# Queries and keys of the second mixer projected with seven products for eight, in a two-layer diffusion backbone

## What is computed

```python
mod = silu(c) @ w_mod + b_mod                 # 1024 x 6144, for c and for c_ctx
h = x * (1 + sc1) + sh1
qa, ka, va, qb, kb, vb, qc, kc, vc = split(h @ w_in)   # nine parts, one matrix
oa, ob, oc = diff_attend(qa, ka, va), neighbourhood_attend(qb, kb, vb), gqa_attend(qc, kc, vc)
ga, gb, gc = split(sigmoid(h @ w_gate + b_gate))
y = (ga * (oa @ w_br[0]) + gb * (ob @ w_br[1]) + gc * (oc @ w_br[2])) @ w_o
x = layernorm(alpha * x + g1 * y); then a mixture of experts, and layernorm again
```

## Time and profile before

| | us |
|---|---|
| median of 3 runs | 2131.27 (2130.95 to 2136.01) |
| profiled execution | 2136.38 |
| its span | 2134.3 |
| PE busy | 2007.2 (94%) |
| DVE busy | 1292.1 (61%) |
| granted clock of TensorE, mean | 0.984 |

### The profile page before, as it was taken

The page is one execution under the profiler, slowest core; times in us unless marked ns, Lnnn a source line. Parts: engine busy times, 40 slices in busy tenths (PEclk is TensorE's granted clock), DMA queues, the critical chain, the costliest instruction groups (busy, mean ns, idle before and its releaser), DMA issues. The chain is left out here.

```text
span 2134.3 us, 25339 instructions
## 1 busy us (share of the span) xinstructions
PE 2007.2 (94%) x9546; PEld 1173.9 (55%) x9546; DVE 1292.1 (61%) x2031; ACT 513.9 (24%) x1007; POOL 238.2 (11%) x250
## 2 busy tenths in 40 slices
PE   7999999999999999699899999999999999979995
PEld 3457766566467754344244676656755676434432
DVE  2747747675456665756444574776744665866664
ACT  2114401143124400122130342003402342002221
POOL 1000020421110000100120002031101000010003
PEclk9999999999999999899999999999999999989998
DMA  7631046411120061689781111552111105238996
GB/s 284 243 118 40 21 143 222 138 55 44 40 82 21 33 279 79 247 341 362 257 278 48 64 41 64 195 185 87 48 57 46 43 21 221 105 133 322 385 350 199
DMA packets 62682, 317.00 MB, mean 149 GB/s; under 512 B 14824, under 2 KB 15280, under 8 KB 34272
## 3 DMA queue, kind: packets, MB, share of 16 engines
q1 hardware_dynamic: 32688, 232.41, 28.9%
q0 software_dynamic: 13136, 53.64, 7.7%
q10 hardware_dynamic: 16736, 29.32, 3.8%
HBM read 286.70 MB, written 27.07 MB: 147 GB/s over the span
## 5 line engine op out<-in xcount | busy, mean ns | idle before, releaser
L1217 PE MATMUL ps<-ring,hT 128*128 128x512 f32 (+1 forms) x960 | 388.4, 560 | 4.0 <-DVE hT L2190 2.0
L1217 PE MATMUL ps<-ring,zT 128*128 128x512 f32 (+2 forms) x992 | 317.5, 600 | 2.0 <-ACT zT L2093 2.0
L1217 PE MATMUL ps<-R,ring 128*128 128x512 f32 (+2 forms) x1024 | 292.3, 437 | 6.3 <-DVE zT L2522 3.5
L1217 PEld LDWEIGHTS ps<-ring,hT 128*128 128x128 f32 x960 | 179.4, 191 | 187.4 <-issue 176.7
L1217 PE MATMUL ps<-hT,ring 128*128 128x320 f32 x896 | 260.5, 436 | 0.0
L1217 PEld LDWEIGHTS ps<-R,ring 128*128 128x128 f32 x1024 | 161.9, 191 | 118.0 <-issue 92.8
L1217 PEld LDWEIGHTS ps<-ring,zT 128*128 128x128 f32 (+2 forms) x992 | 121.5, 156 | 149.0 <-issue 146.4
L1217 PEld LDWEIGHTS ps<-hT,ring 128*128 128x128 f32 x896 | 164.8, 190 | 65.2 <-issue 2.6
L2370 DVE SCALAR_TENSOR_TENSOR R<-ring,cs,R 128x2048 f32<-128x2048 f32 x70 | 173.3, 2476 | 8.3 <-DMA ring<-in_wall 5.5
L2025 ACT COPY R<-ps 128x512 f32<-128x512 f32 (+2 forms) x170 | 96.1, 565 | 271.3 <-PE ps L1506 253.8
L1445 PE MATMUL ps<-R 64*128 64x128 f32 (+2 forms) x992 | 123.2, 374 | 5.7 <-ACT R L1896 2.5
(11 more groups left out here) (335 smaller groups left out, 2460.8 us busy)
## 6 DMA issues: line engine op xcount, KB each, us to landing
ring<-in_wall SPq DMA_DIRECT2D x188, 1024.0 KB, 6.0
hT<-in_wall SPq DMA_DIRECT2D x20, 1024.0 KB, 8.9
y_all<-R ACTq DMA_DIRECT2D x27, 512.0 KB, 6.9
R<-in_wall SPq DMA_DIRECT2D x10, 1024.0 KB, 9.0
R<-in_rows POOLq DMA_DIRECT2D x2, 4096.0 KB, 17.9
R<-mrows POOLq DMA_DIRECT2D x16, 512.0 KB, 21.5
R<-in_x ACTq DMA_DIRECT2D x10, 512.0 KB, 8.9
h_rows<-R ACTq DMA_DIRECT2D x10, 512.0 KB, 2.6
```

The lines of the kernel that those rows point to most:

```text
L1217: ins = nc.tensor.matmul(out, w, m, start=start, stop=stop, **kw)
```

## The change

Chunks 3 and 4 are now computed by the same scheme of seven products: four pairs of output tiles (`TURNED_PAIRS`), each with seven products of four steps in seven separate uses of six PSUM banks (`TURNED_BANKS`). GpSimd makes the four weight sums of a pair (`sum_turned`), in place or in free state, alternating between two sets. ScalarE copies the first product and the sum with the third, VectorE adds the others (`add_turned`, six additions). The token differences are those of the first mixer in `SG`.

The second mixer's gates need them afterwards in the kept slots: six transfers from GpSimd's queue now copy them there, where `token_sum` computed them. ScalarE waits for the transfers before it writes to `SG`.

Group 1 of the modulation gets an accumulator of its own (`first_acc`). Its first seven half passes are made in the merge of the first mixer, 20 more between the additions of the turned products, and the remaining five of group 2 behind them. The pieces' order is 4 behind chunk 3 and 4 behind chunk 4. Its sum is taken after the last turned pair.

The gates' weight sums are now taken one at a time (`one_sum`), at most two per slot of the attention, after an earlier product than before; the fourth is written into the weights themselves.

```diff
@@ -54,6 +54,8 @@
 ADDS = 6
 SUMS = 4
 SIGMOIDS = 3
+DIFFERENCES = 6
+MOST_SUMS = 2
 PIECE = 2048
 FAR = -1e30
 TIE = 1e-30
@@ -62,11 +64,12 @@
 MOD_GROUPS = D * 6 // 2048
 CHUNKS = {0: (2, 0, 1), 1: (3, 4, 5), 2: (6, 7)}
 CHUNK_TYPE = ("q", "k", "v", "q", "k", "v", "q", "kv")
-MOD_ORDER = ((2, 6, 0), (0, 0, 8))
-MOD_SUMS = ((4, 1), (5, 3))
+MOD_ORDER = ((4, 4, 0), (0, 0, 8))
+MOD_SUMS = ((4, 3), (5, 3))
+FIRST_SUMMED = 3
 NEXT_PASSES = {(2, 0): (0, 1, 2), (0, 0): (3,), (0, 1): (4,), (0, 2): (5,), (0, 3): (6,), (1, 0): (7,)}
 NEXT_SUM, NEXT_TURN, NEXT_COPY = (1, 1), (1, 2), (1, 3)
-PROJECT_SLOTS = (0, 1, 2, 3, 4, 5) + 3 * (2, 3) + (0, 1) + 4 * (2, 3)
+PROJECT_SLOTS = (0, 1, 2, 3, 2, 3, 4, 5, 2, 3, 2, 3, 0, 1) + 4 * (2, 3)
 def wall_order():
...
+TURNED_PAIRS = 4
+TURNED_BANKS = (2, 3, 2, 4, 5, 0, 1)
 def units(c):
...
     cross_sum = sb("cross_sum", [128, 4, 128])
+    turned_sums = [[a.rearrange("p (k n) -> p k n", k=4) for a in (area(13824, 512), area(14336, 512), area(17664, 512))],
+           [cross_sum[:], *(a.rearrange("p (k n) -> p k n", k=4) for a in (area(12800, 512), area(13312, 512)))]]
     cexp = area(18176, KB * 32).rearrange("p (k n) -> p k n", k=KB)
     lnst = area(26112, 16 * NT).rearrange("p (t a) -> p t a", t=NT)
...
@@ -626,23 +631,48 @@
     class SumsDone:
-      def __init__(self, first, last):
-        self.first, self.last, self.done = first, last, [[0, 0] for _ in range(3)]
-      def upto(self, br, n):
-        done = self.done[br]
-        while True:
-          a, b = done
-          if a > b:
-            if SEVEN * b + CROSS + 1 > n:
-              return
-            self.last(br, b)
-            done[1] += 1
-          else:
-            if a == PAIRS or (a and SEVEN * (a - 1) + LATE + 1 > n):
...
+        while most and self.done[br] < SUMS * PAIRS:
+          p, j = divmod(self.done[br], SUMS)
+          if n < (SEVEN * p + LOW_LOW + 1 if j == SUMS - 1 else SEVEN * (p - 1) + ACROSS + 1 if p else 0):
+            return
+          self.one(br, p, j)
+          self.done[br] += 1
+          most -= 1
+    def turned_pieces(layer, q):
...
             for dst, a, b in token_halves(layer, br, j):
               ch.step(nc.gpsimd.tensor_tensor(dst, a, b, ALU.subtract), g_tok)
+          def sum_turned(q):
+            for i in turned_pieces(layer, q):
+              pool.wait_ge(full[slot_of(layer, i)], 16 * loads_by(layer, i))
+            if q >= 2:
+              pool.wait_ge(pe_acc, turned_no(q - 2, HIGH_HIGH))
+            (a11, a12), (a21, a22) = turned_weights(layer, q)
+            both, cross, far = turned_sums[q % 2]
+            ch.step(nc.gpsimd.tensor_tensor(both, a21, a22, ALU.add), g_turn)
+            ch.step(nc.gpsimd.tensor_tensor(cross, both, a11, ALU.subtract), g_turn)
...
@@ -1082,9 +1125,15 @@
               if layer == 0:
                 zero_row = y_all[0:1, :].rearrange("r (p n) -> (r p) n", p=8)
                 pool.dma_start(zero_row, MB[0:8, 0, MB_ZERO[0]:MB_ZERO[0] + 128]).then_inc(zero_out, 16)
+              sum_turned(0)
+              pool.wait_ge(pe_gate, gate_no(0, PAIRS - 1, LATE))
               for g in range(LAT):
                 masked_bias(0, g)
+              pool.wait_ge(v_z, KB)
+              sum_turned(1)
               load_bias(1)
...
@@ -1098,12 +1147,13 @@
                 n = pieces.index((layer, ("in", 4, 1)))
                 pool.wait_ge(freed, taken_by(layer, n)[1])
                 for j in range(4):
-                  token_sum(1, j)
-              i = PU.index((br, c, CTX))
+                  for k0, k1, dst in token_rows(layer, 1, j):
+                    pool.dma_start(dst, token_rows(layer, 0, j)[0][2][:, 320 * k0:320 * k1]).then_inc(t_moved, 16)
+              i = PU.index((br, c, 0 if turned(c) else CTX))
               typ = CHUNK_TYPE[c]
               if typ == "k" and turned(c):
-                pool.wait_ge(a_copy, AU.index(PU.index((br, c, units(c) - 1))) + 1)
+                pool.wait_ge(v_turn, turned_adds(TURNED_PAIRS - 1, HIGH_HIGH))
                 pool.dma_start(OUT["bk"][layer].rearrange("p (b t) -> p b t", b=4), KT[:, :, LTOK:TOK]).then_inc(new_k_out, 16)
                 pool.wait_ge(new_k_out, 16 * (br + 1))
...
+          def turned_pair(q):
+            for h in range(2):
+              take("in", h)
+            (a11, a12), (a21, a22) = turned_weights(layer, q)
+            both, cross, far = turned_sums[q % 2]
+            copied = AU.index(PU.index((1, 3, 0))) + 2 * q
+            for o in range(SEVEN):
+              if o == LOW_LOW:
+                if q:
+                  pe.wait_ge(a_copy, copied)
+                weights, tokens = a11, lambda k: hT[:, k, early]
+              elif o == CROSS:
+                if q:
+                  pe.wait_ge(v_turn, turned_adds(q - 1, CROSS))
+                pe.wait_ge(g_turn, SUMS * q + 2)
+                weights, tokens = cross, lambda k: token_row(layer, 0, 1, k)
+              elif o == HIGH_LOW:
+                pe.wait_ge(a_copy, copied + 1)
+                weights, tokens = a12, lambda k: hT[:, 4 + k, early]
+              elif o == DOWN:
+                if q:
+                  pe.wait_ge(v_turn, turned_adds(q - 1, DOWN))
+                pe.wait_ge(g_turn, SUMS * q + 3)
+                weights, tokens = a21, lambda k: token_row(layer, 0, 2, k)
+              elif o == ACROSS:
+                if q:
+                  pe.wait_ge(v_turn, turned_adds(q - 1, ACROSS))
+                weights, tokens = both, lambda k: token_row(layer, 0, 0, k)
+              elif o == LATE:
+                if q:
+                  pe.wait_ge(v_turn, turned_adds(q - 1, LATE))
+                else:
+                  pe.wait_ge(v_z, KB)
+                pe.wait_ge(g_turn, SUMS * q + 4)
+                weights, tokens = far, lambda k: hT[:, 4 + k, late]
+              else:
+                if q:
+                  pe.wait_ge(v_turn, turned_adds(q - 1, HIGH_HIGH))
+                weights, tokens = a22, lambda k: token_row(layer, 0, 3, k)
+              for k in range(STEPS):
+                last = mm(ps[:, TURNED_BANKS[o], 0:320], weights[:, k, :], tokens(k), k == 0 and o != HIGH_LOW, k == STEPS - 1,
+                     frees=k < STEPS - 1, skip_group_check=o in (LOW_LOW, HIGH_LOW))
+              last.then_inc(pe_acc, 1)
...
+                used(2)
+                continue
               for t in range(units(c)):
                 i = PU.index((br, c, t))
-                if br and (n, t) == (0, 2):
+                if br == 2 and (n, t) == (0, 2):
                   pe.wait_ge(v_z, KB * br)
-                if i >= 4:
...
+                  else:
+                    pe.wait_ge(v_turn, turned_adds(TURNED_PAIRS - 1, (CROSS, LATE, HIGH_HIGH)[t - 1]))
+                elif i >= 4:
                   if i - 4 in AU:
                     pe.wait_ge(a_copy, AU.index(i - 4) + 1)
...
@@ -1397,8 +1499,8 @@
                   if br or p:
                     pe.wait_ge(v_part, adds_by(br, p, LOW_LOW))
                   pe.wait_ge(g_sum, SUMS * (PAIRS * br + p) + 2)
-                  if br:
-                    pe.wait_ge(g_tok, sums_ready(br, 1))
+                  if br == 1:
...
                   pe.wait_ge(g_sum, SUMS * (PAIRS * br + p) + 3)
-                  if br:
-                    pe.wait_ge(g_tok, sums_ready(br, 2))
                 weights, tokens = w[:, k, 128:256], token_row(layer, br, 2, k)
               elif o == ACROSS:
                 if k == 0:
                   pe.wait_ge(a_sg, SIGMOIDS * (PAIRS * br + p) + 1)
-                  if br:
-                    pe.wait_ge(g_tok, sums_ready(br, 0))
                 weights, tokens = part_sum[:, k, :], token_row(layer, br, 0, k)
               elif o == LATE:
                 if k == 0:
                   pe.wait_ge(v_part, adds_by(br, p, DOWN))
                   pe.wait_ge(g_sum, SUMS * (PAIRS * br + p) + 4)
-                weights, tokens = cross_sum[:, k, :], hT[:, 4 + k, 320:640]
...
                   if t + 1 == CTX:
                     gate_lambda()
                 if i in AU:
-                  act.wait_ge(pe_acc, i + 1)
+                  if turned(c):
+                    q = TILE_PAIRS * (c - 3) + t // 2
...
@@ -1922,8 +2026,7 @@
                   if br == 2 and c == 6:
                     pass
                   elif turned(c):
-                    b, part = divmod(t, 2)
-                    dst, src = (QT if c == 3 else KT)[:, b, 320 * part:320 * part + 320], ps[:, bank_of(i), 0:320]
+                    dst, src = turned_quarters(q)[(3, 0)[t % 2]], ps[:, TURNED_BANKS[LOW_LOW], 0:320]
...
@@ -1979,6 +2082,8 @@
                     act.wait_ge(v_z, 2 * KB)
                   if layer and br == 1:
                     act.wait_ge(x_out, 16)
...
@@ -2282,12 +2387,18 @@
           def project(br):
             if br == 1:
-              modulation_partials()
+              for q in range(TURNED_PAIRS):
+                for o in (CROSS, DOWN, ACROSS, LATE, HIGH_HIGH):
```

(67 more changed lines are left out.)

86 lines of the change are left out of this document (61 added, 25 removed).

## The result

The changed kernel takes 2110.78 us (median of 4 runs, 2106.84 to 2116.13), the kernel before 2131.79 beside it: a ratio of 0.9899 with an interval of 0.9873 to 0.9925: 1% faster, which is small but clear of the noise. The forecast was 2110, with a range of 2103 to 2114. The profiled execution took 2111.26 us (span 2109.5, mean granted clock 0.983) where the sum had said 2114.6. So the medians are 21.0 us apart and the profiled executions 25.1.

The account below looks back on a forecast made before the run. TensorE was taken as the bound, busy 71.00 of 71.00 us in the second mixer's query and key projection. 2136.4 - 17.2 - 5.6 + 1.0 = 2114.6 us profiled; 21.8 off the 2131.3 median gave 2110, range 2103 to 2114 (wider: 2124).

Parts of the forecast that it names:

- Seven products: Second mixer's query and key projection: 16 fewer TensorE steps of 0.538 us, saving 8.6 us per layer, 17.2 in all.
- GpSimd's sums: Four weight sums per turned pair on GpSimd: 7.7 us taken, 5 to 14.4 possible, at no cost in time.
- VectorE's lateness: VectorE's additions in the turned projection: 9 to 13 us late at the third pair, 0.5 us stall per layer.
- The weights' queue: Next modulation piece lands 41 us after the turned projection starts; VectorE waits up to 7 us, its addition done at 42 to 45.
- Passes' end: VectorE's passes end 83 to 86 us after the turned projection starts, 4 us before TensorE needs the second modulation group's sum.
- Transfers: Six token-difference transfers, 2.6 MB, land 89 us after the turned projection starts, hidden with 10 us of cover.
- rival 2: Token-difference transfers land late, stalling the first gate products 8 to 9 us per layer: 2127 us; chance 0.06.
- Gate sums: Attentions of the three mixers: earlier gate weight sums remove TensorE waits, 2.8 us per layer, 5.6 in all, bounds 0 and 7.6.
- The rule on the shared port: VectorE and GpSimd lock a shared SBUF port: each sum costs VectorE its full 1.26 us, total 1 us higher.
- rival 1: VectorE falls behind the turned products, TensorE stops 3 to 8 us per layer: 2114 to 2125 us; chance 0.19.
- Rival 4: VectorE passes beside GpSimd's sums take 4.86 us throughout, stalling the turned projection 27 us per layer: 2164 us; chance 0.09.
- Rival 3: Turned projection is not the bound; a wait for merging or weights comes up: 2125 to 2137 us; chance 0.04.

Follow-up runs that it names:

- six-pass kernel: The changed kernel with six half passes of VectorE per pair of turned products instead of five: 2113.0 us, ratio 0.9901.
- 10 a pair: The changed kernel with 10 half passes of VectorE per pair of turned products instead of five: 2170.62 us, ratio 1.0174.

## Why the prediction was right, step by step

**Seven products.** Sum 17.2 us, measured 17.45 (8.72 + 8.73). The step kept its price of 0.538 us. No wait came up in its place, and with the old gate sums the same 8.7 us stay.

**GpSimd's sums.** Forecast 1.9 us each, bounds 1.26 and 3.6. Beside passes they took 3.20, near the upper bound, and the other way round they cost VectorE 0.37 us each (0.72 for one) and not 1.0. Both terms were mis-sized, in opposite ways. The third and fourth pair's sums took 10.9 and 8.5 us instead of 7.7. Nothing came of it, since two sums have 17 us.

**VectorE's lateness.** Forecast 9 to 13 us at the third pair with a stall of 0.5 per layer, measured 8.0 at the end and no stall. The first reason is the 0.37 us. At its last addition of the four pairs VectorE was 3.8, 5.3, 8.0 and 8.0 us late, where the prediction's first count had 3, 7 and 11. What brought it from 5.3 to 7.6 us was the wait for the piece. The six-pass kernel confirms the cover. There, two more passes of 2.38 us and one more addition stand between the piece and the addition for which the last product waits: 8.0 + 2 x 2.38 + 0.52, and 0.49 of that addition itself, are 13.8 us, 0.9 above the cover of 12.9. Measured: the product started 0.9 us behind TensorE's pace (0.49 of it in the bracket), and the whole stage took 1.02 more.

**The weights' queue** was right: piece at T0 + 41 (40.8), a wait of up to 7 us (4.83), addition done at T0 + 42 to 45 (42.6).

**The merge** keeps its pace: with a pass of 2.77 us in the gap VectorE is still idle for 0.70 us before the next channel. In all kernels with five passes or fewer the stage is 98.49 us.

**Passes' end** at T0 + 83 to 86, measured T0 + 84.6, with 5.3 us in hand instead of 4 (TensorE's bundle came at T0 + 89.9).

**Transfers** landed by T0 + 89, as forecast; rival 2, which had the rate of the smaller ones, falls. Up to ScalarE's copy of the first gate product, the first reader (404.10), and up to the cross product the cover was 13 us.

**Gate sums.** This term was mis-sized: 5.6 us forecast, 8.0 measured in the three stages, of which the sums alone give 7.6. The first mixer gave 0.8 per layer as said. The second gave 1.9 and 2.6 instead of 1.6; the wait of 1.56 us is gone, and in layer 1 two smaller ones (0.35 and 0.32 us) that are no part of the sums: with the new sums alone they stay, with the seven products alone they go. The third was forecast at 1.4 - 1.0 = 0.4 and gave 0.8 to 1.1, but by another way: the price at its first slot was 2.2 us of waits for 2.07, and the gain came from the copy at 671.85, which I had missed in the waits because it stands with a line of the attention and not of the gates. The upper bound of 7.6 was reached by the sums alone and passed by the whole term; it counted only the gates' own waits.

**The sum.** Of the 3.3 us between 2114.6 and 2111.26, 2.4 are the term of the gate sums (some 0.5 of them layer 1's two waits), 1.0 the missing stall and 0.25 the products; against that go 0.2 in the value tiles and 1.2 at the start, and the rest of the kernel and the edges of the span give 1.1 back. That the median came within 1 us of 2110 is luck in part: the errors go both ways, and the profiled execution before lay 5 us above its median, the one after only 0.5, while the forecast had taken the same 5 us off. (The wider range should have ended at 2125, where rival 1 ends, and not at 2124.)

**The rule on the shared port.** The prediction had set it against the trace: each sum would cost VectorE its full 1.26 us. In this chain it cost 0.37. The 3.20 us of GpSimd's sum agree with the rule's exclusive lock held for a whole instruction (the Trainium skill, SBUF — State Buffer, "SBUF: two separate sides"), since it fits a sum that waits out a pass: the one at 321.78 would wait until the pass that started at 321.13 ends, at 323.85, and with its own 1.26 us end at 325.1; it ended at 325.0. VectorE's side agrees less: it pays a third of what it would. The forecast had also left out that 0.56 us of a sum can run between two passes, while VectorE makes its addition from PSUM; that leaves 1.26 - 0.56 = 0.70 us by an estimate from the rows, and 0.37 were measured.

**Rivals.** Rival 1's lateness does turn into stalls, but from the sixth pass on, and with the wait for the modulation piece as a part of it; at five the kernel is below that point. Rival 4 wanted 4.86 us for each pass beside GpSimd and 2.72 were measured; a VectorE that late by its own passes, at 10 a pair, did end slower than before. Rival 3 falls with the unbroken row of products.

**Open:** 0.3 us of the second mixer's gain in each layer, why layer 1's two small waits went with the seven products, and what an earlier modulation piece would give. No version tried beats the changed kernel by more than the intervals.

## What to carry to other kernels

When a stage's bound hands work to an engine that was nearly full, ask for the cover in microseconds rather than for its share of busy time: here one more pass per pair cost 1 us and two cost 10. Count in that cover the waits of the engine itself: more than half of VectorE's lateness here was a wait for a load. Short operations put between others cost where they stand ahead of a link of a chain, so look through the waits of all consumers of that engine, not only of those that read the operation's result. A part that moves no time (the transfers) can still be what holds the slack for another.

## What the hardware showed that I had not expected

- GpSimd and VectorE do not share the loss evenly. Beside half passes with short PSUM additions between them, a 128x512 sum of GpSimd took 3.20 us instead of 1.27, and a pass 2.72 instead of 2.35. In the row of passes without additions, a 128x1280 subtraction of GpSimd took 4.8 us and cost a pass 2.5.
- Behind a long stop TensorE's matmuls ran at the lower clock, so a stop cost more than its length. The granted clock was 0.50 behind 10.08 us, 0.67 behind 2.88 us and 0.60 behind 2.13 us. Behind single stops of 0.49, 1.25 and 1.81 us it stayed 1.00, and so it did in one case behind 3.40 us (with 10 passes, layer 1; in layer 0 it was 0.50 behind the same stop).
- Smaller GpSimd operations wait less each: 1.48 us for 128x128 (0.51 alone), with passes of 2.45 us. For a whole sum this is dearer (5.92 us instead of 3.20).
- Six transfers within SBUF, 2.6 MB issued in 3.2 us beside the loads of weights, landed in 7.7 to 11.9 us. Those of 256 and 128 KB had taken 10.3 and 10.6 in the kernel before: the larger ones were not slower.
